# Two transformer blocks in one kernel: every fourth pair of weight slots loaded in three transfers

## The reference

```python
def first_block(x, ...):            # 1 layer
    z = rmsnorm(x) @ w_in           # 1024 -> 6704, cut into twelve parts
    y_rnn  = rg_lru(causal_conv(xr)) * gelu(gr)
    y_attn = nsa(q, compress(kc), compress(vc), ksl, vsl, kw, vw, g_nsa)
    x = x + rmsnorm((sigmoid(gm_rnn) * y_rnn + sigmoid(gm_attn) * y_attn) @ w_out)
    x = x + rmsnorm((silu(gate) * up) @ ffn_w_down)       # gate, up = rmsnorm(x) @ ffn_w_gate_up
    return x + sigmoid(x @ ple_w_gate + b) * (p @ ple_w_proj)

def second_block(x, mem, ...):      # 2 layers: gated linear attention, then dilated attention
    for l in range(2):
        y = concat(mix(x), memory_attention(x, mem)) @ w_out[l]
        x = layer_norm(alpha * x + y)
        x = layer_norm(alpha * x + peer(x, ...))

def peer(x, w_q, sub_keys, u, v):
    expert, gate = top 16 of each of 8 heads              # 128 experts for each token
    h = einsum('td,thkd->thk', x, u[expert])
    return einsum('thk,thkd->td', gelu(h) * gate, v[expert])
```

## Time and profile before

| | |
|---|---|
| median of 3 runs | 2068.95 us (2067.94 to 2071.73) |
| profiled execution, its own time | 2069.58 us |
| its span | 2067.8 us |
| TensorE, matmuls | busy 1892.6 us, 92% |
| VectorE, ScalarE, GpSimd | 67%, 43%, 30% |
| bytes moved | 710.15 MB, mean 343 GB/s |
| of it gathers and others of GpSimd's queue | 550.15 MB |
| of it SP's queue | 158.34 MB |

### The profile page before, as it was taken

One profiled execution on the slowest core, in us unless ns is written; L12 is line 12 of the kernel. 1 busy time (PEld: TensorE's weight loads), 2 busy tenths in 40 slices (PEclk: granted clock), 3 DMA queues, 4 the chain that ended last, 5 costly groups with the idle time before them and its releaser, 6 DMA issues. The chain is left out here.

```text
span 2067.8 us, 24840 instructions
## 1 busy us (share of the span) xinstructions
PE 1892.6 (92%) x8012; PEld 1166.3 (56%) x8012; DVE 1382.4 (67%) x2957; ACT 897.1 (43%) x2417; POOL 617.6 (30%) x563
## 2 busy tenths in 40 slices
PE   8999999999998999988999998889999999777776
PEld 7888678887955654432565534456564455222222
DVE  7778566666738767775865645667765575985444
ACT  5657454454634433333434623333454334343332
POOL 0002200000004444344433344333334334444442
PEclk9999999999999999999999999999999999999999
DMA  6633555544549999999999999999999999999996
GB/s 239 223 134 112 204 194 187 195 168 167 220 153 376 421 420 421 421 421 422 419 421 421 413 422 420 421 417 410 421 413 403 415 421 416 422 421 422 421 419 280
DMA packets 99373, 710.15 MB, mean 343 GB/s; under 512 B 11040, under 2 KB 11184, under 8 KB 14384
## 3 DMA queue, kind: packets, MB, share of 16 engines
q0 software_dynamic: 76928, 550.15, 64.5%
q1 hardware_dynamic: 22176, 158.34, 20.3%
q10 hardware_dynamic: 144, 0.11, 0.0%
HBM read 707.51 MB, written 1.05 MB: 343 GB/s over the span
## 5 line engine op out<-in xcount | busy, mean ns | idle before, releaser
L1453 PE MATMUL bank<-arena 128*128 128x512 f32 x2048 | 980.0, 608 | 151.2 <-ACT arena L2085 149.4
L2531 DVE SCALAR_TENSOR_TENSOR arena<-arena,x_tok 128x1024 f32<-128x1024 f32 x512 | 626.9, 1226 | 468.0 <-DMA arena<-peer_uv,arena 462.6
L2241 POOL DMA_INDIRECT arena<-peer_uv,arena x512 | 584.6, 1142 | 868.8 <-PE bank L1453 623.0
L1453 PEld LDWEIGHTS bank<-arena 128*128 128x128 f32 x2048 | 360.8, 190 | 645.4 <-ACT arena L2085 356.7
L2078 ACT ACTIVATE arena<-arena 128x1 f32<-128x1 f32 x512 | 103.6, 202 | 836.3 <-DVE arena L2531 835.5
L922 PEld LDWEIGHTS bank<-xT,weight_ring 128*128 128x128 f32 x1376 | 182.6, 193 | 41.5 <-issue 34.9
L2085 ACT ACTIVATE arena<-arena 128x128 f32<-128x128 f32 x512 | 197.7, 386 | 0.5
L2072 ACT ACTIVATE arena<-const_tile,arena 128x128 f32<-128x128 f32 x512 | 197.8, 386 | 0.0
L922 PE MATMUL bank<-xT,weight_ring 128*128 128x128 f32 (+1 forms) x1376 | 195.0, 294 | 0.8 <-DVE xT L2268 0.8
L922 PE MATMUL bank<-x_low_high,z_high 128*128 128x512 f32 (+1 forms) x480 | 135.9, 351 | 0.0
L1198 PE MATMUL bank<-x_split,w_split 128*128 128x512 f32 x704 | 127.6, 339 | 2.6 <-DVE x_split L2811 2.6
(11 more groups left out here) (321 smaller groups left out, 1990.3 us busy)
## 6 DMA issues: line engine op xcount, KB each, us to landing
weight_ring<-weights SPq DMA_DIRECT2D x149, 1024.0 KB, 4.9
arena<-peer_uv,arena POOLq DMA_INDIRECT x512, 15.1
row_ring<-rows_in POOLq DMA_DIRECT2D x8, 512.0 KB, 4.5
arena<-weights POOLq DMA_DIRECT2D x5, 512.0 KB, 7.7
kept_keys<-weights POOLq DMA_DIRECT2D x4, 512.0 KB, 9.6
const_tile<-consts POOLq DMA_DIRECT2D x1, 1657.0 KB, 8.9
x_tok<-x_in SPq DMA_DIRECT2D x2, 512.0 KB, 4.6
memT<-memT_in POOLq DMA_DIRECT2D x1, 1024.0 KB, 7.2
```

The lines of the kernel that those rows point to most:

```text
L1453: ins = pe.matmul(b[:, :], diag[n % DIAGS], gbuf[n % GBUF][:, 1, h * 512:(h + 1) * 512], start=n % P == 0, stop=n % P == P - 1)
L2241: pool.indirect_dma_start(gbuf[n % GBUF].rearrange("p a d -> p (a d)"), None, peer_uv, bass.IndirectOffsetOnAxis(ap=expert[t][:, s:s + 1]. ...
L2531: dve.scalar_tensor_tensor(u, u, 1.0, x[:, t, :], ALU.mult, ALU.mult, accum_out=hdot[:, s:s + 1])\
```

## The change

SP loads every fourth pair, the one whose place in the ring is the last (`APART_PAIR`, place 3 of 0 to 3), in three transfers in place of one: the pair's first slot whole (128 partitions x 4 KB), of its second slot the first 120 partitions (`APART_ROWS` = 128 - 8), and the last 8 partitions. All three raise `weights_loaded3`, by 16 each, so who reads a slot of this place waits for 48 a round in place of 16; `wait_loaded` holds that count, and all five waits now call it. The other three pairs of a round, and the pair behind the loop, are loaded as before. Bytes and computation are the same.

```diff
+APART_PAIR = RING // PAIR - 1
+APART_ROWS = P - P // 16
...
+        def wait_loaded(e, n):
+
+            s = n % RING // PAIR
+            e.wait_ge(sem(f"weights_loaded{s}"), (48 if s == APART_PAIR else 16) * (n // RING + 1))
...
-                pe.wait_ge(sem(f"weights_loaded{n % RING // PAIR}"), 16 * (n // RING + 1))
+                wait_loaded(pe, n)
...
+            def load_pair(s, pair):
+
+                if s != APART_PAIR:
+                    sp.dma_start(ring[:, PAIR * s:PAIR * (s + 1), :].rearrange("p a n -> p (a n)"),
+                                 pair.rearrange("a p n -> p (a n)")).then_inc(sem(f"weights_loaded{s}"), 16)
+                    return
+                sp.dma_start(ring[:, PAIR * s, :], pair[:, :, 0:SLOT].rearrange("a p n -> p (a n)"))\
+                  .then_inc(sem(f"weights_loaded{s}"), 16)
+                for rows in (slice(0, APART_ROWS), slice(APART_ROWS, P)):
+                    sp.dma_start(ring[rows, PAIR * s + 1, :], pair[:, rows, SLOT:2 * SLOT].rearrange("a p n -> p (a n)"))\
+                      .then_inc(sem(f"weights_loaded{s}"), 16)
+
             with sp.Fori(0, pairs // per) as i:
                 for s in range(per):
-
                     sp.wait_ge(sem("weight_free"), i * RING + PAIR * (s + 1))
-                    sp.dma_start(ring[:, PAIR * s:PAIR * (s + 1), :].rearrange("p a n -> p (a n)"),
-                                 weights[bass.ds(i * per + s, 1), :, :].rearrange("a p n -> p (a n)"))\
-                      .then_inc(sem(f"weights_loaded{s}"), 16)
+                    load_pair(s, weights[bass.ds(i * per + s, 1), :, :])
             for n in range(pairs // per * per, pairs):
-                s = n % per
                 sp.wait_ge(sem("weight_free"), PAIR * (n + 1))
-                sp.dma_start(ring[:, PAIR * s:PAIR * (s + 1), :].rearrange("p a n -> p (a n)"),
-                             weights[n:n + 1, :, :].rearrange("a p n -> p (a n)")).then_inc(sem(f"weights_loaded{s}"), 16)
+                load_pair(n % per, weights[n:n + 1, :, :])
```

More of the change, by code:

```diff
@@ L1761, in start_high @@
                     act.wait_ge(sem("weight_free"), RING + split_no(i - SPLITS) + 1)
-                act.wait_ge(sem(f"weights_loaded{slot % RING // PAIR}"), 16 * (slot // RING + 1))
+                wait_loaded(act, slot)
                 done(act.activation(z_high[:, i % SPLITS, :], ring[:, slot % RING, :], ACT.Copy, scale=scale), "z_high")
```

## The result

The changed kernel takes 2107.49 us (median of 4 runs, 2105.01 to 2110.41) against 2068.44 us of the kernel before measured beside it: 39 us slower, a ratio of 1.018 with a 95% interval of 1.0167 to 1.0194. The forecast was 2062.0 us, range 2055.5 to 2071.5.

A forecast was written before the change was run, and what follows sets the result against it. TensorE was taken to pace the front half (some 640 us), transfers the long rest, each gather timed by one late engine. 2069.58 - 5.7 + 2.0 - 3.6 = 2062.3 us, or 2061.7 from the median; stated 2062.0, range 2055.5 to 2071.5.

The forecast's parts named there:

- A 4 KB row is half of 0.31 us, 0.155 us: In fourth pairs' split transfers: a 4 KB row takes one engine 0.155 us, half of an 8 KB row's 0.31 us.
- What the late engine loses or gains: Transfer-bound half: per fourth pair one engine does 1.24 us less, eight do 0.155 us more, seven the same.
- one engine's 16.1 us: Transfer-bound half: 13 fourth pairs at 1.24 us each take 16.1 us of work off a single engine.
- A's sign: Experiments' theory: loss comes from which on-chip partitions an engine writes; strided at least 20 us under neighbours, 2077 to 2095 us.
- The split over fifteen engines: SP's queue: 120 rows go to fifteen engines, eight rows each, one engine carrying none; 27763 packets.
- rival 2: SP's fourth pairs: the 120 rows go to eight engines, 15 each; slower, 2080 or 2085 us; chance 0.06.
- The tail, -5.7 + 2.0 us: End of transfers: the lone last engine's 5.7 us lead goes, eight others' extra rows add 2.0 us; -3.7 us.
- The 0.06 stretch: Last microseconds of transfer, one engine of 16 busy until about 2056.1 us; gone if the forecast holds, all dry within 2 to 3 us.
- rival 1: End of transfers: an engine other than the late one is relieved; time stays 2069 or becomes 2071 us; chance 0.22.
- The holes, -3.6 us: Transfer-bound loop: 10.8 us of transfer time unused in slices under 422 GB/s; a third of it regained, -3.6 us.
- SP's issues, 0: SP's queue: two more issues per fourth pair hold SP up by 0.7 us; taken as 0 in the sum.
- Rival 3: Long half: weights arrive late, making the kernel slower; chance 0.03.

The follow-up runs named there:

- 16 x 8 neighbouring partitions: Against the kernel before: every fourth pair's first slot whole, its second slot in 16 transfers of 8 neighbouring partitions each; 2168.1 us, one run.
- The strided run: Against the kernel before: every fourth pair's first slot whole, its second slot in 16 transfers of 8 partitions four apart; 2173.22 us, one run.

## Why the prediction was wrong

**What bounds the kernel** was read rightly: the long half goes by its transfers, at 421 GB/s, while TensorE's granted clock is 0.9 or more in every slice. The loss came in there, at the fourth pairs.

**The step that failed** is "A 4 KB row is half of 0.31 us, 0.155 us", under "What the late engine loses or gains". For transfers of 128 rows of 4 KB it held in time: with two and three transfers a pair the long half grew by 0.6 and 1.7 us. Where 120 and 8 rows, or 64 and 64, were written on the chip it didn't: +32.0 and +29.2 us. SP's packets took 496 us more in the change; if all of that lies in the 37 x 128 rows in question, such a row took by my estimate some 0.26 us in place of 0.155 (496 / 4736 on top). And, which no term of the sum had, the gathers' rows beside them took 398 us more. In the prediction's terms the transfer work of the long half, put at no change beyond one engine's 16.1 us, grew by 32.0 us for all. I priced a row by its bytes, whatever the shape of its transfer. SP's 154 transfers (22176 packets) and the gathers of the trace before all have 128 rows, so it held no price for another shape, and I put no bound on it.

Why such a row is slow, the runs don't show. They show where it is: on the chip with 120 and 8 rows (+32.0 us) and with 64 and 64 (+29.2), not with 128 (+0.6 and +1.7), not with 120 rows to main memory (+15.6, against +16.5 with 128), and more with 16 x 8 neighbouring partitions (+85.9) than with 16 x 8 strided ones (+40.7). The 45 us between the last two go with the partitions that a transfer writes, which is A's sign, from one run each; how 120 rows are dealt out, and which engine writes which partitions, isn't shown. The strided run doesn't settle it: SP's issues took 0.65 us in place of 0.28, and its own 40.7 us are unexplained. The prediction had not asked which engine writes which partitions.

**The split over fifteen engines** was right, to the packet (27763), and rival 2 (eight engines) was refuted by it.

**The tail, -5.7 + 2.0 us:** nothing of it came; the choice that carried the forecast, that the relieved engine is the late one, was wrong too. The 0.06 stretch stands, by the prediction's own sign the picture of rival 1, that another engine is the late one. The 120 rows to main memory bear this out from the other side: fifteen engines got 16.1 us more, the long half grew by 15.6 and not by 10.4, and one engine ended alone. So the engine that 120 rows leave out is not late by its queue. Whether the late engine is one of the other fifteen or lateness isn't a matter of load at all stays open; the two runs of 16 transfers, which didn't end with eight engines, speak for the second, if those eight were the same each time.

**The holes, -3.6 us:** mis-sized from the start, and of the wrong sign. The 88 / 422 x 51.7 = 10.8 us were read as time in which engines ran dry. Cut into windows of 1 us from 660 to 2040, the trace before has only 8 with a share under 0.9, and together they lack 1.8 us; the rest of the 10.8 is windows with a full share and fewer GB/s, as 1400 to 1600 already showed (1.01 at 411). In the changed kernel it is 18 windows and 2.9 us: the holes didn't close, and the level fell. A hole (a share of 0.56) and a slow stretch (a share of 1.01 at 372 GB/s) are different things; only the first is starvation.

**SP's issues, 0:** right. In the long half nothing waits for weights. In the front half the changed kernel is 6.6 us later at the first dot product, and ScalarE's waits in the three groups shown grew from 26.3 to 32.3 us. But three whole transfers, with the same number of issues, are 2.7 us sooner there, and the whole pair as 120 and 8, with one issue fewer, is 6.5 us later (one execution each): this loss too seems to go with the shape of the transfers.

**The two added transfers**, by themselves, didn't matter: three of 128 rows took 2070.43 us, at most 3 us more (the upper end, 1.0016).

**Rival 3**, weights late in the long half, priced at 0.03, was refuted: the waits of the long half have none for weights. How long a fourth pair took to land there isn't shown. None of the rivals held the mechanism of the loss; the sum of the slower chances, 0.09, was too low for a transfer shape that the trace had never shown.

## What to carry to other kernels

When a transfer to the on-chip memory gets a shape that the trace doesn't hold (other than all 128 partitions), don't price it by bytes (here half a megabyte in 120 and 8 rows cost 2.5 us more than in whole pairs, in 64 and 64 rows 2.2): try it by itself, beside the traffic it will run with. A share near 1 with fewer GB/s (here 1.01 at 372, against 421) was the mark of slow rows, and the number of packets and the queue's share of the span, both on the page, tell whose. An engine that ends alone is no proof that a given change takes rows off it (a share of 0.06 stood at the end before and after). And before a run is read as load on some engines, count its packets: here 8 and 15 rows of a contiguous block were spread over all sixteen engines, and only the packets said so (26944 in both runs).

## What the runs showed of the hardware

- A transfer of 120 rows of 4 KB from SP ran on fifteen engines, one of 8 rows to the on-chip memory on eight, one of 64 rows on sixteen (packets 27763, 31648 and 28096).
- A transfer of 8 or 15 whole rows of 8 KB, contiguous at both ends in main memory, ran on sixteen engines in 16 equal pieces (26944 packets in both runs).
- Half a megabyte written on the chip in transfers of 120 and 8, or of 64 and 64 partitions cost 2.5 and 2.2 us beside the gathers (+32.0 and +29.2 us in the long half, 13 fourth pairs) over what the same bytes cost in the kernel before, and the gathers' own packets took longer (21340 to 21738 and 21681 us); to main memory 120 rows cost +15.6 us where 128 cost +16.5, and the gathers' packets stayed at 21325 us.
- An even load of 8.1, 15.1 and 16.1 us on every engine, estimated from the 0.31 us of an 8 KB row, lengthened the long half by 8.1, 14.2 and 16.4 us. One engine ended alone for four to six microseconds (a share of 0.06 to 0.08 at 25 to 33 GB/s) in every run looked at, with even and uneven loads.
- An issue on SP of 8 partitions four apart took 0.65 us, of 8 neighbours 0.28 us.
